# A decoder trunk's shared expert: its down products move from the end of each expert loop into the loop

## The reference, cut to what matters

```python
scores = sigmoid(x2 @ w_router); idx = top_k(scores + router_bias, 6)
gate = scores[idx] / sum(scores[idx]) * 2.5
for each token t, each chosen expert e:                # 64 experts of width 256
    acc[t] += gate[t, e] * ((silu(x[t] @ w_gate[e]) * (x[t] @ w_up[e])) @ w_down[e])
shared = (silu(x2 @ w_sh_gate) * (x2 @ w_sh_up)) @ w_sh_down
x = layer_norm(ALPHA * x + acc + shared, ln2_g, ln2_b)  # ALPHA = 4 ** 0.25
```

## Time and profile before

| | |
|---|---|
| median of 3 runs | 1962.34 us |
| the profiled execution's own time | 1960.34 us |
| its span in the profile | 1958.6 us |
| TensorE busy, mean granted clock | 1788.3 us (91%), 0.98 |
| VectorE, ScalarE, GpSimd busy | 749.4, 384.5, 354.6 us |
| moved by the DMA engines | 541.80 MB, 277 GB/s over the span |
| first expert loop and ending | about 384 to 937 us |
| second expert loop and ending | about 1404 us to the end |

### The profile page before, as it was taken

One profiled execution on the slowest core, in us unless ns is written; L12 is line 12 of the kernel. 1 busy time (PEld: TensorE's weight loads), 2 busy tenths in 40 slices (PEclk: granted clock), 3 DMA queues, 4 the chain that ended last, 5 costly groups with the idle time before them and its releaser, 6 DMA issues. The chain is left out here.

```text
span 1958.6 us, 36214 instructions
## 1 busy us (share of the span) xinstructions
PE 1788.3 (91%) x12636; PEld 1106.6 (57%) x12637; DVE 749.4 (38%) x2168; ACT 384.5 (20%) x882; POOL 354.6 (18%) x450
## 2 busy tenths in 40 slices
PE   9999999899998989879999969999889999997877
PEld 7888445456665555543444438754456666664442
DVE  4222754633332323224255553516623333332225
ACT  2112651011111111102265243211011111110001
POOL 8442000011111111110012712200011111111110
PEclk9999999999999999999899989999999999999999
DMA  6220225599999999999122220206899999999997
GB/s 228 79 82 23 97 90 218 213 411 421 421 421 421 421 422 420 421 421 354 55 65 76 65 42 3 70 19 260 327 413 415 422 421 421 420 421 422 422 416 307
DMA packets 144184, 541.80 MB, mean 277 GB/s; under 512 B 31030, under 2 KB 68498, under 8 KB 94302
## 3 DMA queue, kind: packets, MB, share of 16 engines
q1 hardware_dynamic: 122782, 490.20, 62.5%
q0 software_dynamic: 21312, 50.37, 6.6%
HBM read 521.58 MB, written 46.14 MB: 290 GB/s over the span
## 5 line engine op out<-in xcount | busy, mean ns | idle before, releaser
L718 PE MATMUL bank<-W,XT 128*64 128x256 f32 x2880 | 326.6, 383 | 36.9 <-DMA W<-in_w_exp_up_dram 17.8
L718 PEld LDWEIGHTS bank<-W,XT 128*64 128x64 f32 x2880 | 233.9, 138 | 139.9 <-DMA W<-in_w_exp_gate_dram 28.9
L755 PE MATMUL bank<-W,ht 128*64 128x512 f32 x720 | 166.1, 602 | 13.1 <-DMA W<-in_w_exp_down_dram 8.3
L2256 PE MATMUL bank<-XT,room 128*128 128x512 f32 x352 | 158.6, 605 | 0.0
L729 DVE TENSOR_TENSOR sig<-sig,bank 128x256 f32<-128x256 f32 x72 | 30.3, 421 | 268.1 <-ACT sig L725 234.6
L718 PE MATMUL bank<-room,XT 128*64 128x256 f32 x864 | 103.2, 391 | 15.6 <-DMA room<-in_w_exp_gate_dram 7.8
L731 DVE TENSOR_TENSOR h<-sig,bank 128x256 f32<-128x256 f32 x72 | 30.4, 422 | 214.9 <-PE bank L718 214.9
L2256 PEld LDWEIGHTS bank<-XT,room 128*128 128x128 f32 x352 | 66.2, 193 | 82.1 <-issue 81.9
L784 POOL DMA_INDIRECT y_rows<-y,row x36 | 36.7, 1020 | 419.0 <-DVE y L777 419.0
L784 POOL DMA_INDIRECT y_rows<-XT,row x36 | 36.4, 1010 | 412.2 <-DVE XT L777 412.2
L704 ACT ACTIVATE XT<-bank 128x512 f32<-128x512 f32 x74 | 44.2, 597 | 329.8 <-PE bank L696 329.8
(11 more groups left out here) (490 smaller groups left out, 2780.1 us busy)
## 6 DMA issues: line engine op xcount, KB each, us to landing
W<-in_w_exp_gate_dram SPq DMA_DIRECT2D x88, 1024.0 KB
W<-in_w_exp_up_dram SPq DMA_DIRECT2D x88, 1024.0 KB
W<-in_w_exp_down_dram SPq DMA_DIRECT2D x88, 1024.0 KB
room<-in_w_exp_gate_dram SPq DMA_DIRECT2D x40, 1024.0 KB
third_high<-in_w_exp_down_dram SPq DMA_DIRECT2D x40, 1024.0 KB
W<-y_rows SPq DMA_DIRECT2D x24, 1024.0 KB, 13.4
third_up<-in_w_exp_up_dram SPq DMA_DIRECT2D x20, 1024.0 KB
w_shg<-in_w_exp_up_dram SPq DMA_DIRECT2D x20, 1024.0 KB
```

What stands on the lines that cost most here:

```text
L718: last = pe.matmul((gate, up)[m][64 * a:64 * a + 64, :], xt[s][:, k, 64 * a:64 * a + 64], weights(w, a, m)[:, k * FE:(k + 1) * FE], start= ...
L755: last = pe.matmul(B[5 + half][64 * a:64 * a + 64, :], ht[:, j, 64 * a:64 * a + 64], weights(w, a, 2)[:, at:at + 512], start=(j == 0), sto ...
L2256: last = pe.matmul(main(i)[:], wc[i % WBUFS][:, kb, :], K.XT[:, kb, :], start=(kb == 0), stop=(kb == KD - 1))
```

## The change

It does five things.

1. The shared expert's down product is cut into 16 units of 128 tokens by 256 columns. One unit runs in each turn's pass u = 1, on TensorE between the gate and the up products, into bank 5. VectorE adds it to X at once, and multiplies that piece of X by ALPHA in the same instruction. With 18 turns and 16 units, a table K.due holds 0 for the first two turns and 1 for the others: ScalarE stages the unit's hidden values times that number and makes the factor (ALPHA or 1).
2. The shared down weights are loaded at the start of the loop, ahead of slot 2's down weights, into a tile of their own. A value of the routing stage, plan_turns[1], is read into a register of each engine before the loop.
3. To make room, y becomes one tile instead of two, so keep_y waits for the scatter of the pass before; sig is merged into h; and constants that are needed only while others are made move into the arena.
4. The ending has row products alone. The scaling of X (L1045) goes.
5. The second norm's vectors are loaded as single rows of 4 KB. Four products of one row each spread them over the partitions in banks 4 to 7, between the early and the late row products, and ScalarE copies them to SBUF in the middle of its diagonals. TensorE waits for these copies before tile 2.

The core of the diff:

```diff
+UNITS = 16
+UNIT = NT * D // UNITS
...
-    K.upto = sb("upto_f32", [P, P])
-    K.ones = sb("ones_f32", [P, P])
-    K.heads = sb("heads", [P, P])
-    K.masks4 = sb("masks4", [P, 4 * P], BF16)
-    K.level = sb("level", [P, 7, P], BF16)
+    made_in = K.arena[:, 4 * TOKW // P * T:4 * TOKW // P * T + NMH // 2 * T]
+    at = [0]
...
+    K.upto = carve(P, F32)
+    K.heads = sb("heads", [P, P], BF16)
+    K.head_cols = sb("head_cols", [P, 2])
+    K.masks3 = sb("masks3", [P, 3 * P], BF16)
+    K.level = carve(7 * P, BF16).rearrange("p (l t) -> p l t", l=7)
+    K.due = sb("due", [P, MAX_PASSES - UNITS], BF16)
...
-                step.inc(dve.tensor_copy(K.plan_turns[:], gsum[0:1, 0, :]))
+                step.inc(dve.tensor_copy(K.plan_turns[:, 0:1], gsum[0:1, 0, :]))
+                step.inc(dve.tensor_scalar(K.plan_turns[:, 1:2], gsum[0:1, 0, :], -1.0, float(MAX_PASSES // 2), ALU.mult, ALU.add))
...
-        y = [xt_room[:, 0:D], sb("y1", [P, D])[:]]
+        y = xt_room[:, 0:D]
...
-        sig, h = sb("sig", [P, FE]), sb("h", [P, FE])
+        h = sb("h", [P, FE])
...
+        sh_down = sb("w_sh_down_kept", [P, 2 * D])
+        staged_hidden = sb("staged_hidden", [P, 2, P])
+        due, factor = sb("due_now", [P, 1]), sb("factor_now", [P, 1])
+        X_flat = K.X[:].rearrange("p t d -> p (t d)")
...
+            before = eng.value_load(K.plan_turns[0:1, 1:2], min_val=0, max_val=MAX_PASSES // 2 - UNITS)
...
+        def unit_of(turn, before):
+            return (before + turn) & (UNITS - 1)
+
+        def stage_hidden(act, turn, before):
+            wait_from(act, shared_added, turn)
+            act.activation(due[:], K.due[:, bass.ds(before + turn, 1)], ACT.Copy).then_inc(due_kept, 1)
+            act.wait_ge(due_kept, turn + 1)
+            act.activation(factor[:], due[:], ACT.Copy, bias=1.0, scale=ALPHA - 1.0)
+            at = ((before + turn) & (UNITS - D // UNIT)) * (P * UNIT // D)
+            act.activation(staged_hidden[:], shared.hidden[:, :, bass.ds(at, P)], ACT.Copy, scale=due[:, 0:1]).then_inc(hidden_staged, 1)
+
+        def shared_product(pe, n, turn, before):
+            pe.wait_ge(shared.loaded, 16)
+            pe.wait_ge(hidden_staged, turn + 1)
+            pe.wait_ge(y_a, n)
+            at = (unit_of(turn, before) & (D // UNIT - 1)) * UNIT
+            for j in range(2):
+                last = pe.matmul(B[5][:, 0:UNIT], staged_hidden[:, j, :], shared.w[:, j, bass.ds(at, UNIT)], start=(j == 0), stop=(j == 1))
+            last.then_inc(shared_made, 1)
+
+        def add_shared(dve, turn, before):
+            dve.wait_ge(shared_made, turn + 1)
+            x = X_flat[:, bass.ds(unit_of(turn, before) * UNIT, UNIT)]
+            dve.scalar_tensor_tensor(x, x, factor[:], B[5][:, 0:UNIT], ALU.mult, ALU.add).then_inc(shared_added, 1)
...
+                if m == 0 and s == 1:
+                    shared_product(pe, n, shared_turn, before)
...
         def sigmoid(act, n):
-            wait_from(act, hidden_done, n)
+            wait_from(act, h_turned, n)
             act.wait_ge(gate_done, n + 1)
-            act.activation(sig[:], gate, ACT.Sigmoid).then_inc(sigmoid_done, 1)
-
-        def hidden(dve, n, step):
+            act.activation(h[:], gate, ACT.Sigmoid).then_inc(sigmoid_done, 1)
+
+        def hidden(dve, s, n, step, shared_turn, before):
             dve.wait_ge(sigmoid_done, n + 1)
-            step(dve.tensor_tensor(sig[:], sig[:], gate, ALU.mult))
+            step(dve.tensor_tensor(h[:], h[:], gate, ALU.mult))
+            if s == 1:
+                add_shared(dve, shared_turn, before)
             dve.wait_ge(gate_up_done, n + 1)
-            dve.tensor_tensor(h[:], sig[:], up, ALU.mult).then_inc(hidden_done, 1)
+            dve.tensor_tensor(h[:], h[:], up, ALU.mult).then_inc(hidden_done, 1)
...
-        def down(pe, n, turn, w):
+        def down(pe, s, n, turn, w, shared_turn):
+            if s == 1:
+                pe.wait_ge(shared_added, shared_turn + 1)
...
-            wait_from(eng, stored[s], through(n - 2, s))
+            wait_from(eng, stored[1 - s], through(n - 1, 1 - s))
             eng.wait_ge(down_done, 2 * n + 1 + half)
-            dst = y[s][:, half * 512:half * 512 + 512]
+            dst = y[:, half * 512:half * 512 + 512]
...
+                shared.load_down(sp, sh_down[:])
...
+                    if u == 0:
+                        stage_hidden(act, turn, before)
...
+        self.vector_rows = shared.high[0:1, 0:2 * D]
...
     def load_early(self, sp):
-        self.shared.load_down(sp, self.down_room)
-        self.ln.load(sp)
+        for i, src in enumerate(self.ln.src):
+            sp.dma_start(self.vector_rows[:, i * D:(i + 1) * D], src).then_inc(self.ln.loaded, 16)
...
-                                 start=False, stop=(q == ROW_PAIRS - 1))
+                                 start=(q == 0), stop=(q == ROW_PAIRS - 1))
...
-    def products(self, pe):
-        pe.wait_ge(self.shared.loaded, 16)
+    def products(self, pe, y_a, y_d, passes):
         for t in range(2):
-            self.shared_product(pe, t)
             self.row_product(pe, t, 0)
             self.row_product(pe, t, 1)
-        pe.wait_ge(self.scaled, 1)
+        for y_kept in (y_a, y_d):
+            pe.wait_ge(y_kept, 1)
+            pe.wait_ge(y_kept, passes)
+        self.spread_vectors(pe)
         self.row_product(pe, 0, 2)
         self.row_product(pe, 1, 2)
-        self.shared_product(pe, 2)
-        self.row_product(pe, 2, 0)
-        self.row_product(pe, 2, 1)
-        self.row_product(pe, 2, 2)
-        self.shared_product(pe, 3)
+        pe.wait_ge(self.vectors_kept, 4)
+        for q in range(ROW_PAIRS):
+            self.row_product(pe, 2, q)
         self.turn(pe, 0)
         for q in range(ROW_PAIRS):
             self.row_product(pe, 3, q)
         for t in range(1, NT):
             self.turn(pe, t)
 
+    def spread_vectors(self, pe):
+        K = self.K
+        pe.wait_ge(self.ln.loaded, 32)
+        for i in range(4):
+            pe.matmul(K.banks[4 + i][:], K.ident[0:1, 0:1].to_broadcast([1, P]), self.vector_rows[:, i * 512:(i + 1) * 512],
+                      start=True, stop=True).then_inc(self.vectors_spread, 1)
+
+    def keep_vectors(self, act):
+        for i in range(4):
+            act.wait_ge(self.vectors_spread, i + 1)
+            act.activation(self.vectors[:, i * 512:(i + 1) * 512], self.K.banks[4 + i][:], ACT.Copy).then_inc(self.vectors_kept, 1)
...
-            dve.tensor_scalar_mul(X[:, t, :], X[:, t, :], ALPHA).then_inc(self.scaled, 1)
...
+            if n == 2 * ROW_PAIRS - 1:
+                self.keep_vectors(act)
...
-            dve.wait_ge(self.loaded, 32)
+            dve.wait_ge(*(self.ready or (self.loaded, 32)))
```

More of the change, by code:

```diff
@@ L151, in make @@
         step.inc(pool.memset(K.upto[:], 1.0))
-        step.inc(pool.memset(K.ones[:], 1.0))
+        step.inc(pool.memset(K.due[:, 0:MAX_PASSES // 2 - UNITS], 0.0))
+        step.inc(pool.memset(K.due[:, MAX_PASSES // 2 - UNITS:MAX_PASSES - UNITS], 1.0))
         step.inc(pool.memset(K.rank[:], -1.0))
@@ L210, in make @@
             step(pool.tensor_tensor(K.level[:, lv, :], K.level[:, lv, :], K.upto[:], ALU.mult))
-        for q in range(4):
-            step(pool.tensor_copy(K.masks4[:, q * P:(q + 1) * P], (K.upto if q % 2 else K.before)[:]))
+        for q in range(3):
+            step(pool.tensor_copy(K.masks3[:, q * P:(q + 1) * P], (K.before if q % 2 else K.upto)[:]))
         for t in range(NT):
@@ L623, in expert_loop @@
         gates_turned = sem("gates_turned")
+        due_kept, hidden_staged, shared_made, shared_added = (
+            sem(n) for n in ("due_kept", "hidden_staged", "shared_made", "shared_added"))
         steps = sem("steps")
@@ L652, in loop @@
                 for u in range(2):
-                    body(turn * 2 + u, u)
+                    body(turn * 2 + u, u, turn, before)
+        def unit_of(turn, before):
[19 more added lines that the diff above has]
+            dve.scalar_tensor_tensor(x, x, factor[:], B[5][:, 0:UNIT], ALU.mult, ALU.add).then_inc(shared_added, 1)
         def one_hot(dve, s, n):
@@ L706, in keep_xt, with gate_up @@
                 eng.tensor_copy(dst, B[1][:]).then_inc(xt_d, 1)
-        def gate_up(pe, s, n, turn, w):
+        def gate_up(pe, s, n, turn, w, shared_turn, before):
             pe.wait_ge(xt_a, n + 1)
@@ L837, in _, with one_pass @@
                 gather(pool, 1, 1)
-                def one_pass(n, u):
+                def one_pass(n, u, turn, before):
                     read = held(pool, 2 * (n + 1))
@@ L857, in _, with one_pass @@
                 slot_rows(pe, 1, 1)
-                def one_pass(n, u):
+                def one_pass(n, u, shared_turn, before):
                     early = isinstance(n, int)
@@ L864, in from_slot @@
                     def from_slot(w):
-                        gate_up(pe, u, n, turn, w)
+                        gate_up(pe, u, n, turn, w, shared_turn, before)
```

(20 more changed lines are left out.)

19 lines of the change are left out of this document (11 added, 8 removed).

## The result

The changed kernel takes 1973.14 us (median of 20 runs, 1966.75 to 1978.58), the kernel before 1967.55 (20 runs, 1956.79 to 1975.51): ratio 1.0029, 95% interval 1.0018 to 1.0041. Forecast were 1957.7 us and a gain of 4.6. The profiled execution takes 1976.10 us, its span is 1974.4; the one of before was, as the later runs show, 7 us faster than that kernel's median, so the two traces differ by 15.8 us where the medians differ by 5.6.

What follows compares the result with a forecast made beforehand. The prediction took full DMA queues to bound the expert loops, and late TensorE products the endings. Its terms, -9.2 + 3.6 + 0.8 + 0.2 = -4.6 us, gave 1957.7 us by the median, range 1952 to 1967.

Steps and rivals of the forecast that it cites:

- Endings: Both endings after the last scatter: without shared products the row loads bound them; 4.8 and 4.4 us less, 9.2 in all.
- Start of a loop: Shared down weights loaded ahead of two other loads, partly into a dry queue: loads pushed back 0.8 and 1.1 us.
- A unit per turn: TensorE in each of 18 turns: four rows of 256 columns, taken as 1.0 us, bounds 0.85 and 2.0.
- One y: The copy of a pass waits for the scatter before: costs nothing, up to 3 us a pass if a scatter takes 12.
- What the delay does to the queue: Refill after each loop's seventh pass: TensorE's lag shifts the weight stream 3.6 us in the second loop, 0.8 in the first.
- 0.6 + 3.0 = 3.6 us: TensorE's lag at the loops' tightest place: the new table value read, 0.6, and three units, 3.0.
- pauses of TensorE before these passes for no shown reason: Pauses before the tight place: 5.36 and 1.11 us in the second loop, 2.43 in the first.
- Both loops starve: Rival: pauses 3 us longer in both loops shift the weights by 2.6 and 6.6; about 1962.5 us, chance 0.13.
- TensorE becomes bound: Rival: units over 1.76 us a turn make TensorE bound the loops; at 2.5 us a turn, 1980 us; chance 0.07.
- code fetched anew every turn: Rival: longer bodies bring a 5.36 us pause each turn, 77 us a loop, over 2100 us; chance 0.03.

Runs made afterwards that it cites:

- e2: The changed kernel with 186 never-run instructions at the very start of TensorE's program; 1980.3 us (median of 6 runs), ratio 1.0072 to the kernel before.
- e5: The changed kernel without its units in the loops, 40 never-run instructions ahead of TensorE's second loop; 1965.1 us, ratio 0.9984 to the kernel before.
- e8: The kernel of e6 without its never-run instructions, so only its place against the code blocks differs; 1976.5 us, ratio 1.0035 to the kernel before.
- e4: The kernel before once more, unchanged, for comparison and a second trace; 1968.1 us, ratio 0.9999.
- e7: The kernel before with 40 never-run instructions ahead of TensorE's second loop alone; 1960.7 us, ratio 0.9973.
- e1: The kernel before with 62 never-run instructions at the very start of TensorE's program; 1975.8 us, ratio 1.0047.
- e6: The changed kernel, unit's product written once ahead of the odd pass's bodies, loops placed by never-run instructions; 1963.2 us, ratio 0.9980 to the kernel before.

## Why the prediction was wrong, step by step

- *Endings, -9.2.* Right in the mechanism: -8.2 by the trace, with TensorE behind the row loads as foretold. In the second ending of e2, e5 and e8 the last tile begins 26.1 to 26.3 us after the late loads, so the gain there is 2 to 4. That the first ending's gain reaches the second loop is not shown: from the first ending's late loads to that loop it is 503.3, 503.7, 509.1 and 507.0 us with the old ending, 503.5, 507.1, 500.7, 505.9, 503.8 and 504.6 with the new one, means of 505.8 and 504.3.
- *Start of a loop, 0.8 and 1.1.* Not measured. The first refill goes out 6.2 and 5.6 us into the loops (5.6 in both before), but that tells when TensorE is through with a slot, and not how late the loads behind the extra one are.
- *A unit per turn, 1.0.* 1.32: inside the bounds, and over the 0.9 to 1.1 that was to show the prediction right. From the gate products' start to the up products' end it is 8.31 us instead of 7.11, 1.20 of the 1.32.
- *One y, nothing.* No wait for a scatter shows; a small price is not excluded (e5).
- *What the delay does to the queue, 3.6 and 0.8: this is the step that failed.* Its model held: the refill after the seventh pass is the tight place, the first loop has 4.0 us in hand, the second none, and what is late there is late at the loop's end. The lag that went into it, "0.6 + 3.0 = 3.6 us", was 15.2 and 11.3. It counted what the change adds to TensorE's work and took the "pauses of TensorE before these passes for no shown reason" as given, the same after as before. They had a reason, and the change moves it: longer bodies, other places against the blocks.
- *The rivals.* "Both loops starve" named what happened, pauses longer in both, at a chance of 0.13 and with 3 us, where it was 8 to 12 with the clock (the lags of 11.3 and 15.2 less the 3.6): 1962.5 forecast for it, 1973.1 measured. "TensorE becomes bound" and "code fetched anew every turn" did not happen: a unit stays under the 1.76 us at which the first decides, and no packet of code comes after the fifth pass.
- *Traces and medians.* By the trace alone the change would cost 15.8 us. 4.4 of these lie between the first ending and the second loop, where the change leaves the work nearly the same: TensorE's clock is 0.85 between 1100 and 1250 us, 0.91 before. In the ten traces the time from the first ending's late loads to the second loop lies between 500.7 and 509.1 us, so such a difference needs no cause in the change. And the kernel before is itself hit in some runs (e4), which its wide spread fits and e7, 6 us faster, bears out. How the 5.6 us of the medians divide between loops and endings stays open. Of the 15.4 us between forecast and median, 5.2 are the starting median of 3 runs.

The Trainium skill ("Runtime: NRT & Kernel Launch", section "Instruction fetch mechanics") says that code comes in 16 KiB blocks of 256 instructions and that a taken branch out of the window waits for a DMA of the target's block. The packets, and the waits of 5.7 to 6.7 us for a block two ahead, agree with that. It also says that the price of entering a block is mostly hidden; the 3.28 us inside the third pass of the first loop differ. The prediction had weighed this rule for every turn and thrown it out by the steady passes; that was right of the turns, and it should have been priced for the first run of each body.

## What to carry to other kernels

A pause "for no shown reason" at the first run of a piece of code is a price that any edit of that code can move, so it belongs into the sum as a range: here 0 to 6.7 us at each long branch, under a full DMA queue. Where a loop holds several variants of a body, count instructions: a branch over the unused ones that crossed one block's end more cost 5.8 and 6.7 us here, where both endings together saved 8.2. And when an edit adds code to a loop, time it at two places of the code before judging the edit.

## What the runs showed of the hardware

- While the weight loads fill the queue, a block that only the branch asks for starts 3.4 to 4.3 us after the branch (444.97 to 448.38, and 1475.34 to 1479.62 in the second loop), takes about 1.0, and TensorE goes on 1.3 to 1.4 us after its end.
- Six bodies with their branches, some 1,290 instructions or about five blocks, stay in place for a whole loop: no packet begins between 453.97 and 936.6 us.
- A pause of 5 us cost more than itself: the granted clock was 0.5 from 452.00 to 458.83 us, the products began again at 453.48, and the pass that followed took 2.6 us longer.
- Instructions that never run moved the time by 8 us (e1), by 6 (e7) and by 11 to 13 (e6, e8).
